# A state-space mixer in one core's layer stack: three stages become one static order of steps

## The reference

```python
zxbcdt = x @ w_in                         # 1024 -> 6176: z 2048, xbc 4096, dt 32
xbc = silu(causal_depthwise_conv(xbc, conv_w, conv_b))      # 4 taps
xs, bm, cm = xbc[:2048], xbc[2048:3072], xbc[3072:]         # 32 heads x 64; 8 groups x 128
dt = softplus(dt_raw + dt_bias);  a = -exp(a_log)
# two chunks of 128 tokens, 8 groups of 4 heads:
a_cum   = cumsum(dt * a)
decay   = exp(where(causal, a_cum[l] - a_cum[s], -inf))
y_diag  = (C B^T * decay) @ (xs * dt)
states  = B^T @ (xs * dt * exp(a_cum[-1] - a_cum))          # handed to the next chunk
y_off   = (C @ states_before) * exp(a_cum)
y = (y_diag + y_off + d_skip * xs) * silu(z)
y = y * rsqrt(mean(y * y, per group of 256) + eps) * norm_w
out = y @ w_out
```

## Time and profile before

| | us |
|---|---|
| median of three runs | 2550.51 |
| the three runs | 2550.09, 2550.51, 2557.11 |
| profiled execution, first to last instruction (span) | 2555.1 |
| of it busy: TensorE | 2156.7 |
| VectorE, ScalarE, GpSimd | 689.0, 316.1, 178.1 |

### The profile page before, as it was taken

The page is one execution under the profiler, slowest core; times in us unless marked ns, Lnnn a source line. Parts: engine busy times, 40 slices in busy tenths (PEclk is TensorE's granted clock), DMA queues, the critical chain, the costliest instruction groups (busy, mean ns, idle before and its releaser), DMA issues. The chain is left out here.

```text
span 2555.1 us, 33386 instructions
## 1 busy us (share of the span) xinstructions
PE 2156.7 (84%) x13513; PEld 1452.7 (57%) x13513; DVE 689.0 (27%) x2072; ACT 316.1 (12%) x843; POOL 178.1 (7%) x240
## 2 busy tenths in 40 slices
PE   8997678988888849769987888749889998988997
PEld 7846446655555524447654555524468844447863
DVE  3407522111111130731111111136622202743211
ACT  2212100000000000400000000001412101132200
POOL 0004200000000010000000000000000200000110
PEclk9996786777777769577777777779799998989999
DMA  9330055999999964146999999773034434303420
GB/s 328 136 138 28 24 174 218 395 395 395 395 394 392 372 251 147 50 167 244 395 395 395 394 395 395 296 269 132 34 120 156 148 129 142 120 34 132 146 101 25
DMA packets 246122, 574.69 MB, mean 225 GB/s; under 512 B 13316, under 2 KB 16634, under 8 KB 245534
## 3 DMA queue, kind: packets, MB, share of 16 engines
q1 hardware_dynamic: 242974, 569.46, 60.5%
q0 software_dynamic: 3072, 4.21, 0.5%
HBM read 568.39 MB, written 9.44 MB: 226 GB/s over the span
## 5 line engine op out<-in xcount | busy, mean ns | idle before, releaser
L856 PE MATMUL ps<-ring,arena 128*32 128x256 f32 x3968 | 300.1, 469 | 103.4 <-DMA ring<-in_moe_w_up_dram 59.1
L1972 PE MATMUL ps<-arena,ring 128*128 128x256 f32 x1408 | 304.4, 380 | 1.6 <-DVE arena L239 1.6
L856 PEld LDWEIGHTS ps<-ring,arena 128*32 128x32 f32 x3968 | 160.5, 135 | 253.8 <-issue 209.7
L261 PE MATMUL ps<-ring,arena 128*128 128x512 f32 x672 | 296.3, 604 | 2.5 <-ACT arena L647 0.9
L1972 PEld LDWEIGHTS ps<-arena,ring 128*128 128x128 f32 x1408 | 267.8, 190 | 38.1 <-DVE arena L239 2.3
L834 PEld LDWEIGHTS ps<-arena,h 128*128 128x128 f32 x2112 | 258.8, 204 | 29.5 <-issue 26.3
L834 PE MATMUL ps<-arena,h 128*128 128x32 f32 x2112 | 266.5, 288 | 2.9 <-DVE arena L824 2.9
L1269 PE MATMUL ps<-ring,arena 128*128 128x512 f32 (+1 forms) x576 | 249.4, 593 | 2.4 <-DVE arena L239 1.6
L896 PE MATMUL ps<-ring,arena 128*32 128x256 f32 x1984 | 211.7, 601 | 37.5 <-issue 36.4
L261 PEld LDWEIGHTS ps<-ring,arena 128*128 128x128 f32 x672 | 130.1, 194 | 165.7 <-issue 161.7
L1269 PEld LDWEIGHTS ps<-ring,arena 128*128 128x128 f32 x576 | 109.7, 192 | 135.0 <-issue 131.4
(11 more groups left out here) (290 smaller groups left out, 1786.5 us busy)
## 6 DMA issues: line engine op xcount, KB each, us to landing
ring<-in_moe_w_gate_dram SPq DMA_DIRECT2D x62, 2048.0 KB, 19.4
ring<-in_moe_w_up_dram SPq DMA_DIRECT2D x62, 2048.0 KB, 22.4
ring<-in_moe_w_down_dram SPq DMA_DIRECT2D x62, 2048.0 KB, 19.8
ring<-in_w_up_dram SPq DMA_DIRECT2D x22, 2048.0 KB, 8.0
ring<-in_ssm_w_in_dram SPq DMA_DIRECT2D x12, 2048.0 KB, 10.4
ring<-in_w_in_dram SPq DMA_DIRECT2D x10, 2048.0 KB, 11.1
ring<-in_w_down_dram SPq DMA_DIRECT2D x10, 2048.0 KB, 7.9
ring<-in_attn_w_qkv_dram SPq DMA_DIRECT2D x6, 2048.0 KB, 19.9
```

Of the source, the lines that this page charges most:

```text
L261: mm = nc.tensor.matmul(ps[:, 4 + 2 * tt + half, :], lhs(4 * i + k, tt), w[:, k, half * 512:(half + 1) * 512], start=(i == 0 and k == 0), ...
L856: mm = nc.tensor.matmul(ps[j * CAP:(j + 1) * CAP, 2 + b, 0:256], xg[:, b, k * CAP:(k + 1) * CAP], w[:, k, (j % 2) * 256:(j % 2 + 1) * 256] ...
L1972: mm = nc.tensor.matmul(ps[:, n % 4, 0:SEQ], w[:, k, k4 * P:(k4 + 1) * P], xT_mlp[:, k, :], start=(k == 0), stop=(k == KD - 1))
```

## The change

The two blocks become one. A list `STEPS` holds 32 convolution tiles, 8 z pieces, the four parts of the step sizes, 8 turns of x and 2 of B, 16 scores, 16 mixes, 8 squares, 4 normalises, 8 turns of y and 16 output pieces; each engine walks through the list and does its share of each step.

- The weight chunks are ordered B, C, x, z, x, z, B, C, x, z, x, z.
- Convolution and z pieces share PSUM banks 0 to 2; turns use bank 3, scores 4 and 5, products 6, turned y 7. Output pieces use 0 to 3.
- silu(v) is computed as (tanh(v/2) + 1) * v/2: the parameters are halved when they are copied, ScalarE takes tanh, and VectorE does one operation more per tile (`conv_silu`) and per z piece (`z_silu`).
- x times dt and x times d are taken by VectorE straight from the turned bank (`use_turned_x`).
- The decay comes from one product per head: GpSimd multiplies a strict lower triangle by a head's step sizes (`step_masks`), TensorE multiplies that with the triangle, and ScalarE takes exp from PSUM. The four operations of L723 per unit are gone.
- Normalise does two groups at once. The first exponent of ScalarE stands ahead of the convolution.
- SyncE issues the rest of the constants before the third chunk, and the norm's parameters without waiting.

```diff
-        c_xbc = [add(cols8(w_in, DI + 512 * i, DI + 512 * i + 512)) for i in range(CONV // 512)]
-        c_z = [add(cols8(w_in, 512 * i, 512 * i + 512)) for i in range(DI // 512)]
+        for kind, i in (("xbc", 4), ("xbc", 6), ("xbc", 0), ("z", 0), ("xbc", 1), ("z", 1), ("xbc", 5), ("xbc", 7),
+                        ("xbc", 2), ("z", 2), ("xbc", 3), ("z", 3)):
...
+        STEPS = [("conv", 16), ("conv", 17), ("conv", 18), ("conv", 19), ("dt", 0),
+                 ("conv", 24), ("dt", 1), ("turn_b", 0), ("conv", 25), ("dt", 2), ("conv", 26), ("conv", 27), ("dt", 3),
+                 ("conv", 0), ("conv", 1), ("conv", 2), ("conv", 3),
+                 ("z", 0, 0), ("turn_x", 0, 0), ("z", 0, 1), ("turn_x", 0, 1), ("score", 0),
+                 ("conv", 4), ("conv", 5), ("conv", 6), ("mix", 0), ("score", 1),
+                 ("conv", 7), ("z", 1, 0), ("mix", 1), ("score", 2), ("turn_x", 1, 0),
...
+                 ("conv", 28), ("square", 1), ("conv", 29), ("normalise", 0), ("turn_b", 1), ("conv", 30), ("turn_y", 0),
+                 ("mix", 4), ("score", 5),
...
+                 ("conv", 12), ("square", 3), ("conv", 13), ("normalise", 1), ("mix", 8), ("score", 9),
+                 ("conv", 14), ("turn_y", 2), ("conv", 15), ("mix", 9), ("score", 10),
...
+                 ("out", 0, 0), ("square", 5), ("out", 0, 1), ("normalise", 2), ("mix", 12), ("score", 13),
...
+                 ("out", 1, 2), ("out", 1, 3), ("mix", 15), ("square", 7), ("normalise", 3),
+                 ("out", 2, 0), ("out", 2, 1), ("out", 2, 2), ("turn_y", 6), ("turn_y", 7), ("out", 2, 3),
+                 ("out", 3, 0), ("out", 3, 1), ("out", 3, 2), ("out", 3, 3)]
...
+                sp.dma_start(cst[:, P:C_ALL], t["constants"][:, P:C_ALL]).then_inc(loaded_c.sem, 16)
                 ring.issue(sp, RING_SLOTS)
-
-                sp.dma_start(cst[:, P:C_ALL], t["constants"][:, P:C_ALL]).then_inc(loaded_c.sem, 16)
-                ring.issue(sp, c_z[-1] + 1 + RING_SLOTS)
-                sp.wait_ge(loaded_c.sem, 16)
+                sp_ln_params(sp, lnp, t["ln_mix_g"][0], t["ln_mix_b"][0])
+                ring.issue(sp, c_wout[-1] + 1 + RING_SLOTS)
...
+                def new_piece(step):
+                    d = piece_at[step]
+                    if d >= 3:
+                        pe.wait_ge(piece_freed.sem, d - 2)
+                    return ps[:, d % 3, :]
...
+                def scores(u):
+                    g, c = u // 2, u % 2
+                    pe.wait_ge(conv_done.sem, conv_through((16 + g, 24 + g)))
+                    pe.wait_ge(steps_in_ready.sem, u + 1)
+                    if u:
+                        pe.wait_ge(cbm_done.sem, u)
+                        pe.wait_ge(decay_ready.sem, u)
...
+                    for r in range(R):
+                        mm = nc.tensor.matmul(ps[:, 5, r * P:(r + 1) * P], steps_in[:, r * P:(r + 1) * P], triu,
+                                              start=True, stop=True)
...
+                def products(u):
+                    g, c = u // 2, u % 2
+                    pe.wait_ge(mixer_ready.sem, u + 1)
+                    pe.wait_ge(turn_freed.sem, max(turn_at["turn_x", g // 2, c], turn_at["turn_b", g // 4]) + 1)
+                    if u:
+                        pe.wait_ge(y_done.sem, u)
...
+                def turn_y(g):
+                    pe.wait_ge(yn_ready.sem, g + 1)
+                    if g:
+                        pe.wait_ge(yT_ready.sem, 2 * g)
...
             def _(act):
                 act.wait_ge(params_copied.sem, 1)
+                act.wait_ge(loaded_dt.sem, 4 * 16)
+                nc.scalar.activation(a_row, dt_rows[:, 1, :], ACT.Exp).then_inc(dt_act.sem, 1)
...
-                    nc.scalar.activation(dst, conv_acc[:, n % 2, :], ACT.Silu).then_inc(conv_done.sem, 1)
+                    nc.scalar.activation(conv_tanh[:, m % 2, :], conv_acc[:, m % 2, :], ACT.Tanh)\
+                        .then_inc(tanh_done.sem, 1)
...
+                def conv_silu(n):
...
+                    nc.vector.scalar_tensor_tensor(conv_dst(n), conv_tanh[:, m % 2, :], 1.0, conv_acc[:, m % 2, :],
+                                                   ALU.add, ALU.mult).then_inc(conv_done.sem, 1)
...
+                def step_masks(u):
+                    g, c = u // 2, u % 2
+                    if u:
+                        pool.wait_ge(scored.sem, u)
+                    nc.gpsimd.tensor_tensor(steps_in.rearrange("p (r s) -> p r s", r=R),
+                                            later.unsqueeze(1).to_broadcast([P, R, P]),
+                                            bcast(dta[:, c, heads4(g)], P), ALU.mult).then_inc(steps_in_ready.sem, 1)
...
+                for u in range(UNITS):
+                    if u % 2 == 0:
+                        end_inputs(u // 2)
+                    mixers(u)
+                    if u + 1 < UNITS:
+                        step_masks(u + 1)
```

More of the change, by code:

```diff
@@ L294, in dve_add_sums @@
                     hs = h[:, tt, half * 512:(half + 1) * 512]
-                    bank = ps[:, 4 + 2 * tt + half, :]
+                    bank = ps[:, first_bank + 2 * tt + half, :]
                     if stats:
@@ new lines, in hybrid_stack @@
+        yT = bcT
+        b_tok = area(12288, G * NST)
+        xdt = area(13312, 2, TT, 512)
+        GW = R * HD
+        steps_in = area(15360, R * P)
+        decay = area(15872, 2, R * P)
+        conv_acc = area(16896, 2, SEQ)
+        conv_tanh = area(17408, 2, SEQ)
+        z_tanh = area(17920, 2, 512)
+        cb_m = area(18944, 2, P)
+        xdt_end = area(19200, GW)
+        state = area(19456, 2, GW)
+        y_off = area(19968, GW)
+        junk = area(20224, GW)
+        later = area(20480, P)
@@ new lines, in _ @@
+                for kind, *s in STEPS:
+                    if kind == "conv":
+                        conv_tile(*s)
+                    elif kind == "z":
+                        z_piece(*s)
+                    elif kind == "dt":
+                        dt_products(*s)
+                    elif kind == "turn_x":
+                        turn_x(*s)
+                    elif kind == "turn_b":
+                        turn_b(*s)
+                    elif kind == "score":
+                        scores(*s)
+                    elif kind == "mix":
+                        products(*s)
+                    elif kind == "turn_y":
+                        turn_y(*s)
+                    elif kind == "out":
+                        out_piece(*s)
@@ new lines, in _ @@
+                open_tile = None
+                for kind, *s in STEPS:
+                    if kind == "conv":
+                        conv_taps(*s)
+                        if open_tile is not None:
+                            conv_silu(open_tile)
+                        open_tile = s[0]
+                    elif open_tile is not None and kind not in ("mix", "square", "normalise"):
+                        conv_silu(open_tile)
+                        open_tile = None
+                    if kind == "z":
+                        z_silu(*s)
+                    elif kind == "dt":
+                        dt_chain(*s)
+                    elif kind == "turn_x":
+                        use_turned_x(*s)
+                    elif kind == "turn_b":
+                        use_turned_b(*s)
+                    elif kind == "score":
+                        mask_scores(*s)
+                    elif kind == "mix":
+                        outputs(*s)
+                    elif kind == "normalise":
+                        normalise(*s)
```

637 lines of the change are left out of this document (325 added, 312 removed).

## The result

| | before | after |
|---|---|---|
| median, us | 2551.01 (2550.09 to 2557.11, 4 runs) | 2483.57 (2475.09 to 2487.65, 4 runs) |
| profiled execution, us | 2557.11 | 2484.86 |
| its span, us | 2555.1 | 2483.1 |
| end of TensorE's mixer work, us | 357.6 | 288.8 (forecast 297.6) |
| VectorE, ScalarE, GpSimd busy in the mixer, us | | 119.1, 61.9, 41.1 (forecast at most 145, 64, 45) |

The ratio is 0.9731 [0.971, 0.9753]: 67 us faster. The forecast was 60 us (0.9764, outside the interval) and 2490.4 us. The mechanism is the forecast's; the gain was 7 to 9 us larger, which puts the result at the lower edge of the range (2483.0): the median just inside it, and 0.9731 of the old median, 2481.9, just outside.

The account below looks back on a forecast made before the run. TensorE was taken to bound the mixer: 279.8 us of work from 12.0, plus stalls 1.6 and 1.0 and handoffs 3.2, ends at 297.6 against 357.7. Saving 60.1 from 2555.1 gives 2495.0, 2490.4 as a median; range 2483 to 2516.

Parts of the forecast that it names:

- TensorE's work in one line at full clock: Mixer: TensorE's products sum to 279.8 us at full clock, ending at 291.8 if it never waits.
- A scan unit at 2.7: Scan: scores and products of one unit take TensorE 2.7 us at full clock; sixteen take 43.2 us.
- Handoffs, 32 of 0.1: Mixer: TensorE loses 0.1 us at each of 32 handoffs, 3.2 us, with ends 0 and 12.8.
- 32 transposes at 0.135: Mixer: turning eight groups of y costs TensorE 32 transposes of 0.135 us, 4.3 us.
- The two stalls: Mixer: TensorE waits 1.6 us at the first turned group and 1.0 us at the last, group 7.
- The chain of a unit is hidden: Scan: a unit's chain through the other engines takes 6.1 us, under TensorE's other work of 8.2 us or more.
- Rival B: Scan: a unit's chain undercounted by 3 us, each unit stalls 1 to 1.6 us, 2506 to 2516 us; chance 0.15.
- The other engines: Mixer: VectorE at most 145 us busy of 286, ScalarE 64, GpSimd 45; none bounds.
- The rule against the change: Mixer: VectorE and GpSimd exclude each other; a sixth of 32 new silu operations meet, some 5 us on VectorE, 0 in sum.
- Tables (C): Mixer: tanh and exp in different tables, 31 us of loads on ScalarE, 5 to 20 us lost, 2495 to 2510; chance 0.05.
- The clock (D): Mixer: small products among the pieces lower the clock; below 0.83 the kernel is slower, at 0.78 it takes 2571; chance 0.05.
- Given back later (E): Expert stage: it waits for weights that do not come earlier, time about 2550 us; chance 0.03.

Follow-up runs that it names:

- no_stalls: The changed kernel with the first turn of y behind the next unit and the last two each before an output piece of its own; 2479.38 us, ratio 0.972.
- the repetition: The changed kernel itself, unedited, timed again on one chip with other kernels; 2484.75 us, ratio 0.973 to the kernel before.
- cover1: The changed kernel with one piece between each unit's scores and its products instead of two or more; 2489.59 us, one run.
- cover0: The changed kernel with each unit's products right behind its scores, no piece between them; 2569.51 us, one run.
- silu_tables: The changed kernel with ScalarE's silu function in place of tanh, VectorE's operation kept to pass the value on; 2481.70 us, one run.
- outs_last: The changed kernel with all 16 output pieces moved to the end of the order; 2504.62 us, one run.
- cover0_busy: As cover0, with six needless products on TensorE between scores and products of units 0 to 11; 2546.25 us, one run.

## Why the prediction was right, and where its size was off

**TensorE's work in one line at full clock.** Right, and this is the mechanism: idle 2.6 us, clock 0.99. From the common start the gain is 328.9 - 262.6 = 66.3 us. Idle time fell by 40.9 - 2.6 = 38.3; the other 28.0 is work that ran at half clock before. The rows agree: the three of the earlier trace rows add up to 304.7 us busy, against 274.2 now, 30.5 less, of which 2.5 are the first tiles. Some two fifths of the gain are the clock. The forecast had it in, since it priced every product at full clock.

**The step that failed is the sum's sizes, and with them the range's lower end.** The forecast let only the stalls and the handoffs vary below its middle and took the price of a scan unit as fixed, so 2483 was its floor. (Without stalls and handoffs its own terms end at 291.8, which is 2484.6 as a median, not 2483.) The work itself was cheaper than the floor allowed. The terms, from 297.6 to 288.8:

- A scan unit at 2.7: measured 2.44 (84.54 to 86.98), 16 x 0.26 = 4.2 less, the largest. I took 0.40 of waiting out of the earlier trace rows, but the scores took 1.12 here against 1.67 there (209.37 to 211.04), so 0.55 had gone beyond the work; the products took 1.32 against 1.40.
- Handoffs, 32 of 0.1: measured 0, by 3.2 us less. All of TensorE's idle time is in the two stalls, and no_stalls has none at all in its 258.0 us. A wait for a result that is already there costs nothing that adds up.
- 32 transposes at 0.135: measured 0.109, 0.8 less. The mean of the earlier trace rows is a busy time over overlapping instructions.
- The first tiles: 176.4 us held a start of 16.6 us, this profile had one of 14.2: 2.5 less. That is chance, not the change; in the repetition it was 15.6.
- The clock behind the first stall: 2.1 more with the 0.4 that stays open, and not foreseen.
- 0.2 us remain untraced.

These are 8.8 us of the profile. Behind the mixer came 3.2 more, which is spread. Against that the forecast took 4.6 us from span to median, and the span of the profile after is only 0.5 below the median: a median 6.8 us under the forecast is the net of these, and that it is just inside the range is luck.

**The two stalls** were forecast at 1.6 and 1.0 and took 1.56 and 1.02, at the places named and for the releasers named.

**The chain of a unit is hidden.** Right in the order as it is, with no wait at any of the 16 products. The cover of 8.2 against a chain of 6.1 could not be read directly. Cover1 shows that a single piece is enough for 14 of 16 units, and that the chain's real length depends on what else is queued on VectorE. Rival B is refuted here, and cover0 shows what it looks like.

**The other engines.** VectorE 119.1 against at most 145, ScalarE 61.9 against 64, GpSimd 41.1 against 45. The bound for VectorE took over the busy time of a stage in which VectorE and GpSimd met. The root's three small operations (72 of them, two columns wide) took 22.8 us there and now, for two groups at once, 5.9 (36 of them, 0.163 each); before, the one that ran beside L683 took 1.12. That is 17 of the 26 us. The adds of L738 are another 6.5: seven of the eight met L683 and took 1.46 each, and they take 0.425 now. One of the root's operations before (timeline):

```profile
227.84 1.12 DVE L210 TENSOR_TENSOR tiny<-tiny 128x2 f32<-128x2 f32 x1
```

**The rule against the change.** From the rule that the two engines' instructions exclude each other (the Trainium skill, SBUF — State Buffer, Who interferes with whom) some 5 us on VectorE were estimated for 32 new silu operations. The trace has one of the 32 beside a GpSimd operation, where a sixth was estimated; it took 0.72, to 0.27 behind the end of GpSimd's mask, and the others 0.42:

```profile
199.61 0.72 DVE L772 SCALAR_TENSOR_TENSOR arena<-arena 128x256 f32<-128x256 f32 x1 [0.48 <-ACT arena L644]
```

```profile
199.02 1.04 POOL L719 TENSOR_TENSOR arena<-arena 128x512 f32<-128x512 f32 x1
```

The trace agrees with the rule here and in the norm (3.24 against 1.22). What was wrong is the estimate of the meetings from a busy share: in this order the two engines' turns lie apart, which is a matter of the list and no certainty.

**Tables (C)**: no load between tanh and exp, and silu_tables shows that loads would have been hidden but for 0.4 us; the price of 5 to 20 us given for C was too high. **The clock (D)**: 0.99, so narrow work among the pieces does it no harm. As a mechanism it was the right one to fear: cover0 is slower than the kernel before, at 0.89 and with 52 us idle. In these kernels the clock fell around waits and not in narrow work. **Given back later (E)**: 536 us of the expert stage show the same rows 69 us earlier.

## What to carry to other kernels

A static order in which TensorE always has a ready piece is worth more than its idle time (28.0 us beside 38.3 here), since the work between waits loses its clock; in the new order the two rewrites of the arithmetic were worth 0.4 and 1.3 us, and the pieces between a scan unit's scores and its products 9 (one left) or 86 (none left). Take the in-line price of a short instruction from start to start in a stretch without waits, and add nothing for handoffs. Two medians a few microseconds apart are compared from a common point of the trace behind the start-up, where the same code differs by 2.6 us.

## What the runs showed of the hardware that was not expected

- A wait of 1.56 us was followed by a stretch at a granted clock of 0.57 over 4 us in the kernel after, and cost 1.7 us beyond itself. It is no rule: of seven profiles with this stall at the first turned group, four have the fall and three (outs_last, cover1, cover0_busy) have not. The stall of 1.02 us at 270.97 brought no such loss: the 20 instructions behind it took 8.58 us, the 0.43 of full clock. In cover0, sixteen waits of 2 to 6.7 us cost 36.4 us of slower work beside 52.2 of idle time.
- Needless products in twelve of those waits, 33.1 us of them, shortened the mixer by 24.2 us.
- The first tiles, the same work in all kernels, took 14.2 to 16.9 us from one profile to the next.
- VectorE's 1024-column add took 3.24 us beside GpSimd and 1.22 alone; four such operations in a row on VectorE were faster than two on each engine, by 1.66 us.
- One VectorE operation in 32 met GpSimd's in the new order, and took 0.72 us for 0.42; before, seven of eight adds did, at 1.46.
- 30 more table loads of 1.283 us on ScalarE, 38.5 us, made the path 0.4 longer.
